# Stick-breaking attention in pairs of heads: both products of the next step made together, and a projection's chunk kept whole behind the turn of the weights

## The chip, the cores and the metric

The kernel runs on one core of a Trainium2 chip. The metric is the device time in microseconds of one launch, and the kernel before is given by the median of three timed runs, 2637.6 us.

## What is computed

The program is one inference step of a two-layer decoder trunk on 1024 prompt tokens and 8 x 4 sample tokens (T = 1056 columns), model width 1024, in float32. Layer 0 mixes tokens with a gated short convolution, layer 1 with stick-breaking attention (16 heads of 64), and each is followed by a convolutional feed-forward block. Only the attention of layer 1 is touched by the change. For one head it is, cut to what matters:

```python
z = q @ k.T / sqrt(64) + bias            # strictly causal: key s < query t
beta, keep = sigmoid(z), sigmoid(-z)
w[t, s] = beta[t, s] * prod(keep[t, j] for s < j < t)
o = w @ v                                # v, k, q are projections of the normalised x
```

## The kernel before, in words

Activations lie with features on partitions and tokens in columns. Every projection is computed in chunks of 352 tokens (TJ = 3 chunks for T). A matrix product in near-float32 precision takes three matmuls per 128 x 128 block of weights (`three`, lines 520, 523 and 524): high by high, low by high, high by low. GpSimd splits each weight tile into these two halves (lines 496 and 498), once the first matmul of the tile that is three places on has counted `w_used`.

The attention runs over 8 pairs of heads. For a pair there are 8 steps s (`STEPS`), one for each block of 128 queries, from the widest (1024 keys at s = 0) to the narrowest (128 keys at s = 7). A step of one head consists of

- `scores` on TensorE (line 705, with the diagonal mask, line 708),
- `sigmoids` on ScalarE, which make beta and keep for head 0 and then for head 1,
- `weigh(s, h)` on VectorE: a running product over keep from the right (a scan, line 1535), and its multiplication into beta (line 1539),
- `turn(s, u)` on TensorE, the transposition of the weights in PSUM (line 738); u = 0 is the first four blocks of keys, u = 1 the rest, which only the wide steps 0 to 3 have (`WIDE`),
- the copies out of PSUM: `copy_first` on ScalarE for u = 0, `copy_second` on VectorE for u = 1 (line 1518),
- `values(s, u)` on TensorE (line 767), the product with v.

TensorE is filled up by the projections of the pair that comes next: it has 9 chunks (`CHUNKS`: three of k, three of q, three of v), each 24 matmuls on eight blocks k = 0..7 of the features, all in PSUM bank 0, and one chunk is put into each step (the last two into step 7). VectorE moves each out of PSUM, scaled, by `take(after, n)` (lines 1507 and 1511), and counts `lin_taken`; the next chunk waits for that count.

All engines run the order in which their instructions are written. TensorE's order in a step s of `attend` is: `scores(s+1)`; `turn_v` for s = 0 or `values(s-1, 1)`; the first half of chunk s; `turn(s, 0)`; the second half of chunk s; `values(s, 0)`; `turn(s, 1)`. VectorE's is: `take(s-1)`; `copy_second(s-1)`; `weigh(s, 1)`; for s = 0 the two copies of v (`copy_v`, line 1524); `weigh(s+1, 0)`. So the product of head 1 of a step is made in the step itself, and that of head 0 one step earlier. `values(s-1, 1)` waits for the semaphore `second_copied`, `turn(s, 0)` for `weighed` of each head. In ScalarE's `sigmoids(s)` keep of head h waits for `scanned` of the same head one step earlier, because there is one buffer `keep` for each head, while beta has two for each.

The last pair (`attend_last`) has no next pair to project. Its steps are filled with the attention of the sample tokens, two samples in every two steps (`sample_scores`, `sample_weigh`, `sample_turn`, `sample_values`, `sample_out`, `sample_take`).

Of the kernel before, what the change touches and what calls it, by code (L numbers as in the profile page):

```python
# [23 lines left out]
KC = D // P  # L24
# [4 lines left out]
TJ = 3  # L29
# [61 lines left out]
H_SC_IN, H_SC_OUT, H_FFN0, H_QKV, H_WO, H_FFN1 = (BLOCKS * n for n in range(6))  # L91
# [15 lines left out]
FIRST_BANK = [0, 1, 2, 3, 4, 5, 0, 1, 2]  # L107
# [17 lines left out]
STEPS = QT  # L125
# [4 lines left out]
CHUNKS = 3 * TJ  # L130
# [43 lines left out]
def build(nc, x_in, weights, taps_sc, taps_ffn, state_sc, state_ffn, gains, bias_heads, bias_rows,  # L174
# [6 lines left out]
    with ctx:  # L181
# [110 lines left out]
        def projected(n):  # L292
            return bank[n // 3][:, n % 3, 0:TW]
# [23 lines left out]
        def sem(name):  # L317
            return ctx.enter_context(nc.semaphore(name))
# [31 lines left out]
        lin_taken = sem("lin_taken")  # L350
# [166 lines left out]
        def _(pe):  # L517
            def three(o, w, c0, hi, lo, first, last, counts=False):

                mm = nc.tensor.matmul(o, w_hi[w][:, c0:c0 + P], hi, start=first, stop=False)  # L520
                if counts:
                    mm.then_inc(w_used, 1)
                nc.tensor.matmul(o, w_hi[w][:, c0:c0 + P], lo, start=False, stop=False)  # L523
                return nc.tensor.matmul(o, w_lo[w][:, c0:c0 + P], hi, start=False, stop=last)  # L524
# [183 lines left out]
                    nc.tensor.matmul(score[h][:, width - P:width], ident_b[:, :], diag_b[:, :],  # L708
                                     start=False, stop=True).then_inc(scored, 1)

            def project(count, n, bank_n, half=None, h_base=None):

                w, j = n // TJ, n % TJ
                ring = (T_QKV + w) % SPLIT
                for k in range(KC) if half is None else range(half * KC // 2, (half + 1) * KC // 2):
                    if k == 0 and j == 0:
                        pe.wait_ge(w_split, count(3, T_QKV + w + (RAW + 1)))
                    if h_base is not None:
                        pe.wait_ge(h_ready, h_base + j * KC + k + 1)
                    mm = three(projected(bank_n), ring, k * P, h_hi[:, k, j * TW:(j + 1) * TW],  # L720
                               h_lo[:, k, j * TW:(j + 1) * TW], k == 0, k == KC - 1, j == k == 0)
                    if k == KC - 1:
                        mm.then_inc(lin_full, 1)
# [47 lines left out]
            def attend(count, after, par):  # L771

                for s in range(STEPS):
                    if s + 1 < STEPS:
                        scores(count, s + 1, par)
                    elif after is not None:
                        pe.wait_ge(lin_taken, after(CHUNKS, 2 * TJ))
                        scores(after, 0, 1 - par)
                    if s == 0:
                        turn_v(count)  # L780
                    elif WIDE[s - 1]:
                        values(count, s - 1, 1)
                    if after is not None:
                        pe.wait_ge(lin_taken, after(CHUNKS, s))
                        project(after, s, 0, 0)
                        if s == STEPS - 1:
                            project(after, s, 0, 1)
                    turn(count, s, 0)
                    if after is not None:
                        if s == STEPS - 1:  # L790
                            pe.wait_ge(lin_taken, after(CHUNKS, STEPS))
                            project(after, STEPS, 0)
                        else:
                            project(after, s, 0, 1)
                    values(count, s, 0)
                    if WIDE[s]:
                        turn(count, s, 1)

            first = pair_count(0)
            for n in range(CHUNKS):  # L800
                if n < RING:
                    pe.wait_ge(block_taken, TAKEN_FFN0 + BLOCKS - RING + n + 1)
                else:
                    pe.wait_ge(lin_taken, n - RING + 1)
                project(first, n, FIRST_BANK[n], None, H_QKV if n < TJ else None)
                if n == 0:
                    fold_mean(2, 1)
                    sum_four(2, QUADS - 1)
                if n == 1:
                    fold_mean(2, 2)  # L810
                if n == 2 * TJ:
                    pe.wait_ge(lin_taken, 2 * TJ)
                    scores(first, 0, 0)
# [447 lines left out]
        def _(dve):  # L1261
# [230 lines left out]
            def take(count, n, par, reuse):  # L1492

                j = n % TJ
                block = slice(j * TW, (j + 1) * TW)
                if reuse is not None and n == 0:
                    dve.wait_ge(k_stored, reuse(16, 16))
                    dve.wait_ge(k_copied, reuse(1, 1))
                if reuse is not None and n == TJ:
                    dve.wait_ge(q_copied, reuse(1, 1))  # L1500
                if reuse is not None and n == 2 * TJ:
                    dve.wait_ge(v_stored, reuse(16, 16))
                    dve.wait_ge(v_copied, reuse(1, 1))
                bank_n = 0 if reuse is not None else FIRST_BANK[n]
                dve.wait_ge(lin_full, count(CHUNKS, n + 1))
                if n // TJ == 1:
                    V.scalar_tensor_tensor(q_t[par][:, block], projected(bank_n), DH ** -0.5, rstd[:, block],
                                           ALU.mult, ALU.mult).then_inc(lin_taken, 1)
                else:
                    dst = k_t[par] if n < TJ else v_t  # L1510
                    V.tensor_tensor(dst[:, block], projected(bank_n), rstd[:, block], ALU.mult).then_inc(lin_taken, 1)
# [15 lines left out]
            def weigh(count, s, h):  # L1527
                n, width, w = 2 * s + h, WIDTH[s], beta[s % 2][h]
                dve.wait_ge(beta_done, count(PER_HEAD, n + 1))
                dve.wait_ge(keep_done, count(PER_HEAD, n + 3))  # L1530

                dve.wait_ge(weighed, count(PER_HEAD, n + 1))

                back = keep[h][:, width - 1:0:-1]
                V.tensor_tensor_scan(prod[:, width - 1:0:-1], back, back, 1.0,  # L1535
                                     ALU.mult, ALU.bypass).then_inc(scanned, 1)
                dve.wait_ge(scanned, count(PER_HEAD, n + 3))

                V.tensor_tensor(w[:, 0:width - 1], w[:, 0:width - 1], prod[:, 1:width],  # L1539
                                ALU.mult).then_inc(weighed, 1)  # L1540

            def attend(count, after, par):
                for s in range(STEPS):
                    if s and after is not None:
                        take(after, s - 1, 1 - par, count)
                    if s and WIDE[s - 1]:
                        copy_second(count, s - 1)
                    weigh(count, s, 1)
                    if s == 0:
                        copy_v(count)  # L1550
                    if s + 1 < STEPS:
                        weigh(count, s + 1, 0)
                    elif after is not None:
                        take(after, s, 1 - par, count)
                        weigh(after, 0, 0)
                        take(after, s + 1, 1 - par, count)

            first = pair_count(0)
            invert(2, 0)
# [8 lines left out]
            weigh(first, 0, 0)  # L1568
            for n in range(CHUNKS - 2, CHUNKS):
                take(first, n, 0, None)  # L1570
            with dve.Fori(0, (KC - 2) // 2) as i:
                for q in range(2):
                    attend(pair_count(i, q), pair_count(i, q + 1), q)
            attend(pair_count(KC - 2), pair_count(KC - 1), 0)

            def sample_q(bp):
# [34 lines left out]
            def attend_last(count):  # L1611
                V.memset(q_rows[:, :], 0.0).then_inc(made, 1)
                for s in range(STEPS):
                    bp = s // 2
                    if s and WIDE[s - 1]:
                        copy_second(count, s - 1)
                    weigh(count, s, 1)
                    if s == 0:
                        copy_v(count)
                        dve.wait_ge(made, 6)  # L1620
                        sample_q(0)
                    elif s % 2 == 0:
                        sample_take(bp - 1)
                        sample_q(bp)
                    if s + 1 < STEPS:
                        weigh(count, s + 1, 0)
                    if s % 2 == 0:
                        sample_weigh(bp)
                sample_take(NB // 2 - 1)
# [114 lines left out]
```

## Time and profile before

| | |
|---|---|
| timed runs | 2636.41, 2637.6, 2638.77 us |
| the profiled execution's own time | 2637.77 us |
| its span, first to last instruction | 2636.0 us |
| mean granted TensorE clock | 0.993 |
| busy in the span: TensorE, VectorE, ScalarE, GpSimd | 98%, 54%, 20%, 27% |
| attention stage, from the first scores to the last output of the samples | about 1193 to 1743 us |

The attention stage is one fifth of the span. Its first seven pairs repeat one pattern of about 66.7 us each; pair 4, from 1392.5 to 1459.3 us, stands for them. A matmul's record lasts longer than the time after which the next may start, so the distance from one start to the next start is what an instruction costs TensorE. Times are microseconds from the start of the span.

### The profile page before, as it was taken

The numbers are of one execution on the slowest core, as the hardware profiler recorded it, in microseconds if no ns is written. First come the engines' busy times: TensorE is split into PE (matmuls) and PEld (weight loads), VectorE is DVE, ScalarE is ACT, GpSimd is POOL, SyncE is SP. The second block draws the span as 40 slices with busy tenths as digits, with TensorE's granted clock in tenths as the row PEclk, the third lists the DMA queues.
The fourth block names the chain that finished last, engine by engine and source line by source line (L and its number), as shares of the span: only waits on it lengthen the run. The fifth ranks groups of instructions, "written<-read, shape, count | busy, mean of one in ns | idle before, by whom it ended". The sixth has DMA issues, their size and how long they took to land.

```text
span 2636.0 us, 40878 instructions
## 1 busy us (share of the span) xinstructions
PE 2577.5 (98%) x16934; PEld 2451.6 (93%) x16934; DVE 1423.8 (54%) x1430; ACT 533.9 (20%) x1081; POOL 719.0 (27%) x408
## 2 busy tenths in 40 slices
PE   7999999999999999999999999989999999999996
PEld 7999999999999999988888888669999999999995
DVE  8333446444444444466777777654644444444445
ACT  4000221000000000144444444432100000000012
POOL 4333333322322233321111111013233232223332
PEclk9999999999999999999999999999999999999998
DMA  4111111111111111121111111731111111111111
GB/s 141 42 48 48 47 43 49 46 43 48 48 33 48 48 48 48 52 97 59 42 41 41 41 41 41 240 123 41 49 48 41 48 48 33 48 49 48 48 44 67
DMA packets 62428, 149.07 MB, mean 57 GB/s; under 512 B 5570, under 2 KB 28866, under 8 KB 62274
## 3 DMA queue, kind: packets, MB, share of 16 engines
q1 hardware_dynamic: 56082, 130.35, 15.4%
q10 hardware_dynamic: 6192, 16.36, 1.6%
q8 instruction: 134, 2.20, 0.3%
q14 instruction: 20, 0.16, 0.0%
HBM read 128.91 MB, written 17.78 MB: 56 GB/s over the span
## 4 chain that ended last, share of the span: by engine, by line
PE 94%; DVE 4%; issue 1%; ACT 1%; DMA 0%; DVEq 0%; ACTq 0%
PE bank L520 28%; PE bank L524 28%; PE bank L523 28%; PE bank L767 3%; PE bank L705 3%; PE bank L738 2%; DVE total L1295 1%; DVE h_lo L1286 1%; PE bank L708 0%; DVE h_lo L1368 0%; PE bank L870 0%; DVE prod L1535 0%; DVE rstd L1300 0%; PE bank L839 0%; DVE y_rows L1362 0%
## 5 line engine op out<-in xcount | busy, mean ns | idle before, releaser
L520 PE MATMUL bank<-h_hi,w_hi 128*128 128x352 f32 x3648 | 1193.3, 327 | 18.9 <-DVE h_lo L1286 9.1
L524 PE MATMUL bank<-h_hi,w_lo 128*128 128x352 f32 x3648 | 1178.9, 323 | 0.0
L523 PE MATMUL bank<-h_lo,w_hi 128*128 128x352 f32 x3648 | 1173.6, 322 | 0.0
L496 POOL CAST w_hi<-raw 128x1024 fp32r<-128x1024 f32 x196 | 221.4, 1130 | 1861.8 <-PE bank L520 1817.7
L520 PEld LDWEIGHTS bank<-h_hi,w_hi 128*128 128x128 f32 x3648 | 686.3, 188 | 30.6 <-issue 20.5
L523 PEld LDWEIGHTS bank<-h_lo,w_hi 128*128 128x128 f32 x3648 | 690.5, 189 | 0.9 <-issue 0.2
L524 PEld LDWEIGHTS bank<-h_hi,w_lo 128*128 128x128 f32 x3648 | 688.0, 189 | 0.0
L498 POOL TENSOR_TENSOR w_lo<-raw,w_hi 128x1024 fp32r<-128x1024 f32 x196 | 486.9, 2484 | 15.7
L1422 DVE TENSOR_TENSOR x<-x,bank 128x1056 f32<-128x1056 f32 x174 | 218.2, 1254 | 321.9 <-PE bank L524 321.9
L520 PE MATMUL bank<-a_hi,w_hi 128*128 128x352 f32 x1056 | 343.4, 325 | 3.1 <-DVE x L1422 3.1
L523 PE MATMUL bank<-a_lo,w_hi 128*128 128x352 f32 x1056 | 340.7, 323 | 0.0
L524 PE MATMUL bank<-a_hi,w_lo 128*128 128x352 f32 x1056 | 340.6, 323 | 0.0
L1399 DVE TENSOR_TENSOR ext<-bank,rstd 128x1056 f32<-128x1056 f32 x44 | 55.4, 1258 | 340.5 <-PE bank L524 340.5
L520 PEld LDWEIGHTS bank<-a_hi,w_hi 128*128 128x128 f32 x1056 | 198.4, 188 | 10.5 <-DVE x L1344 4.0
L1535 DVE TENSOR_TENSOR_SCAN prod<-keep 128x895 f32<-128x895 f32 (+7 forms) x128 | 196.4, 1534 | 16.1 <-ACT keep L916 12.3
L916 ACT ACTIVATE smp<-ext 128x32 f32<-128x32 f32 x52 | 12.0, 231 | 942.3 <-DVE ext L1399 851.6
L523 PEld LDWEIGHTS bank<-a_lo,w_hi 128*128 128x128 f32 x1056 | 198.4, 188 | 0.3
L524 PEld LDWEIGHTS bank<-a_hi,w_lo 128*128 128x128 f32 x1056 | 198.4, 188 | 0.0
L916 ACT ACTIVATE beta<-bank,bias_pair 128x896 f32<-128x896 f32 (+7 forms) x128 | 94.9, 741 | 212.9 <-PE bank L708 208.9
L1539 DVE TENSOR_TENSOR beta<-beta,prod 128x895 f32<-128x895 f32 (+7 forms) x128 | 125.2, 978 | 4.4
L1374 DVE TENSOR_SCALAR y<-ext,tap_ffn 128x1024 f32<-128x1024 f32 x44 | 116.5, 2648 | 9.7 <-DVE ext L1399 9.6
L1381 DVE SCALAR_TENSOR_TENSOR y<-ext,tap_ffn,y 128x1024 f32<-128x1024 f32 x88 | 113.0, 1284 | 0.7 <-DVE y L1388 0.4
(123 smaller groups left out, 1641.7 us busy)
## 6 DMA issues: line engine op xcount, KB each, us to landing
raw<-weights SPq DMA_DIRECT2D x196, 512.0 KB, 3.5
x_spill<-x ACTq DMA_DIRECT2D x8, 528.0 KB, 6.1
k_out<-k_t ACTq DMA_DIRECT2D x8, 528.0 KB, 2.9
v_out<-v_t ACTq DMA_DIRECT2D x8, 528.0 KB, 2.7
x<-x_spill SPq DMA_DIRECT2D x8, 528.0 KB, 7.4
pages_hi<-cache_k SPq DMA_DIRECT2D x8, 512.0 KB, 6.3
pages_hi<-cache_v SPq DMA_DIRECT2D x8, 512.0 KB, 7.5
pages_lo<-cache_k SPq DMA_DIRECT2D x8, 512.0 KB, 7.3
```

The lines of the kernel that those rows point to most:

```text
L496: nc.gpsimd.tensor_copy(w_hi[ring][:, :], raw[slot][:, :]).then_inc(w_high, 1)
L498: nc.gpsimd.tensor_tensor(w_lo[ring][:, :], raw[slot][:, :], w_hi[ring][:, :].bitcast(f32), ALU.subtract).then_inc(w_split, 1)
L520: mm = nc.tensor.matmul(o, w_hi[w][:, c0:c0 + P], hi, start=first, stop=False)
L523: nc.tensor.matmul(o, w_hi[w][:, c0:c0 + P], lo, start=False, stop=False)
L524: return nc.tensor.matmul(o, w_lo[w][:, c0:c0 + P], hi, start=False, stop=last)
L705: nc.tensor.matmul(score[h][:, n0:n1], q_t[par][rows, i * P:(i + 1) * P], k_t[par][rows, n0:n1], start=True, stop=n1 < width)
L916: return nc.scalar.activation(o, i, func, **kw)
L1374: V.tensor_scalar(o[:, 0:SEQ], e[:, 0:SEQ], tap(0), None, ALU.mult).then_inc(tapped, 1)
L1381: main = V.scalar_tensor_tensor(o[:, 0:SEQ], e[:, n:n + SEQ], tap(n), o[:, 0:SEQ], ALU.mult, ALU.add)
L1422: V.tensor_tensor(xx, xx, result(s), ALU.add).then_inc(taken[s], 1)
L1535: V.tensor_tensor_scan(prod[:, width - 1:0:-1], back, back, 1.0, ALU.mult, ALU.bypass).then_inc(scanned, 1)
L1539: V.tensor_tensor(w[:, 0:width - 1], w[:, 0:width - 1], prod[:, 1:width], ALU.mult).then_inc(weighed, 1)
```

## The change

The functions named are those described above. In the diff `chunks` is the range of the blocks k of a chunk.

```diff
-            def project(count, n, bank_n, half=None, h_base=None):
+            def project(count, n, bank_n, chunks=range(KC), h_base=None):
...
-                for k in range(KC) if half is None else range(half * KC // 2, (half + 1) * KC // 2):
+                for k in chunks:
...
                     elif WIDE[s - 1]:
                         values(count, s - 1, 1)
-                    if after is not None:
+                    ahead = {0: 6, STEPS - 1: KC}.get(s, 0)
+                    if ahead:
                         pe.wait_ge(lin_taken, after(CHUNKS, s))
-                        project(after, s, 0, 0)
-                        if s == STEPS - 1:
-                            project(after, s, 0, 1)
+                        project(after, s, 0, range(ahead))
                     turn(count, s, 0)
-                    if after is not None:
-                        if s == STEPS - 1:
-                            pe.wait_ge(lin_taken, after(CHUNKS, STEPS))
-                            project(after, STEPS, 0)
-                        else:
-                            project(after, s, 0, 1)
+                    if s == STEPS - 1:
+                        pe.wait_ge(lin_taken, after(CHUNKS, STEPS))
+                        project(after, STEPS, 0)
+                    else:
+                        if not ahead:
+                            pe.wait_ge(lin_taken, after(CHUNKS, s))
+                        project(after, s, 0, range(ahead, KC))
                     values(count, s, 0)
...
             def attend(count, after, par):
                 for s in range(STEPS):
-                    if s and after is not None:
+                    if s:
                         take(after, s - 1, 1 - par, count)
                     if s and WIDE[s - 1]:
                         copy_second(count, s - 1)
-                    weigh(count, s, 1)
                     if s == 0:
                         copy_v(count)
                     if s + 1 < STEPS:
                         weigh(count, s + 1, 0)
-                    elif after is not None:
+                        weigh(count, s + 1, 1)
+                    else:
                         take(after, s, 1 - par, count)
                         weigh(after, 0, 0)
                         take(after, s + 1, 1 - par, count)
+                        weigh(after, 0, 1)
...
             weigh(first, 0, 0)
             for n in range(CHUNKS - 2, CHUNKS):
                 take(first, n, 0, None)
+            weigh(first, 0, 1)
...
                     if s and WIDE[s - 1]:
                         copy_second(count, s - 1)
-                    weigh(count, s, 1)
...
                     if s + 1 < STEPS:
                         weigh(count, s + 1, 0)
+                        weigh(count, s + 1, 1)
                     if s % 2 == 0:
                         sample_weigh(bp)
```

On VectorE `weigh(s+1, 1)` now follows `weigh(s+1, 0)` in step s, where `weigh(s, 1)` used to stand at the head of step s. On TensorE the chunk of a step is no longer halved around `turn(s, 0)`: in step 0 three quarters stand ahead of it and a quarter behind, in steps 1 to 6 the whole chunk stands behind, and step 7 is as before. In the last pair only VectorE's order changes.

## Rows read from the trace of the kernel before

**Rows 1.** Windows, pair 4: length, PE, PEld, DVE, ACT, POOL busy, clock, DMA, GB/s.

```profile
1392.60:1459.40 66.80, 66.12 (x508) 55.15 (x507) 49.56 (x52) 30.16 (x54) 11.75 (x6) 1.00 0.12 41
```

**Rows 2.** Waits of PE in 1192 to 1743: total us, times, longest.

```profile
PE bank L738 <- DVE v_rows L1524: 5.1, 8, 2.4
...
PE bank L738 <- DVE beta L1539: 2.3, 4, 0.9
...
PE bank L767 <- DVE w_second L1518: 0.2, 1, 0.2
```

**Rows 3.** Timeline of PE, pair 4: start, us, line, operation, count, idle before.

```profile
1406.30 0.40 PE L520 MATMUL bank<-h_hi,w_hi 128*128 128x352 f32 x1
...
1408.73 1.06 PE L738 MATMUL bank<-ident,beta 128*128 128x128 f32 x8 [0.28 <-DVE v_rows L1524]
...
1411.64 1.09 PE L767 MATMUL bank<-w_first,v_rows 128*64 128x128 f32 x16
...
1415.44 1.09 PE L767 MATMUL bank<-w_second,v_rows 128*64 128x128 f32 x16
...
1432.02 1.13 PE L705 MATMUL bank<-k_t,q_t 64*128 64x512 f32 x4
...
1441.25 0.44 PE L767 MATMUL bank<-w_second,v_rows 128*64 128x128 f32 x4
```

**Rows 4.** Windows of PE on one whole chunk and two halves.

```profile
1399.24:1403.30 4.06, 3.96 (x16) 1.00 0.00 0
1416.47:1418.49 2.02, 2.02 (x8) 1.00 0.03 8
1419.29:1421.37 2.08, 1.99 (x8) 1.00 0.00 0
```

**Rows 5.** Timeline of DVE, pair 4, steps 0 and 1.

```profile
1408.50 4.13 DVE L1535 TENSOR_TENSOR_SCAN prod<-keep 128x895 f32<-128x895 f32 x1
...
1413.68 0.52 DVE L1511 TENSOR_TENSOR k_t<-bank,rstd 128x352 f32<-128x352 f32 x1
1414.11 1.27 DVE L1518 COPY w_second<-bank 128x512 f32<-128x512 f32 x2
1415.31 2.01 DVE L1535 TENSOR_TENSOR_SCAN prod<-keep 128x895 f32<-128x895 f32 x1
1417.35 1.09 DVE L1539 TENSOR_TENSOR beta<-beta,prod 128x895 f32<-128x895 f32 x1
```

**Rows 6.** Timeline of ACT, pair 4: the first copy of step 0, keep of step 4.

```profile
1409.39 1.09 ACT L916 ACTIVATE w_first<-bank 128x512 f32<-128x512 f32 x2
...
1434.01 0.68 ACT L916 ACTIVATE keep<-bank,bias_pair 128x512 f32<-128x512 f32 x1
```

**Rows 7.** Timeline of POOL, pair 4.

```profile
1408.37 2.38 POOL L498 TENSOR_TENSOR w_lo<-raw,w_hi 128x1024 fp32r<-128x1024 f32 x1
1434.49 1.33 POOL L496 CAST w_hi<-raw 128x1024 fp32r<-128x1024 f32 x1 [23.73 <-PE bank L520]
1435.90 3.18 POOL L498 TENSOR_TENSOR w_lo<-raw,w_hi 128x1024 fp32r<-128x1024 f32 x1
```

**Rows 8.** Timeline of DVE, pair 4, the products of step 4, head 0.

```profile
1435.02 1.87 DVE L1535 TENSOR_TENSOR_SCAN prod<-keep 128x511 f32<-128x511 f32 x1
1436.93 2.70 DVE L1539 TENSOR_TENSOR beta<-beta,prod 128x511 f32<-128x511 f32 x1
```

**Rows 9.** Windows of PE around idle times: length, busy, granted clock, DMA, GB/s.

```profile
43.05:46.00 2.95, 0.00 (x0) 0.92 0.45 150
46.00:48.95 2.95, 2.92 (x8) 0.50 0.07 28
1674.60:1676.90 2.30, 0.00 (x0) 1.00 1.06 389
1676.90:1680.50 3.60, 3.55 (x28) 0.53 1.05 406
...
55.50:60.00 4.50, 3.02 (x19) 1.00 0.01 4
```

More of the change, by code:

```diff
@@ L804, in _ @@
                     pe.wait_ge(lin_taken, n - RING + 1)
-                project(first, n, FIRST_BANK[n], None, H_QKV if n < TJ else None)
+                project(first, n, FIRST_BANK[n], h_base=H_QKV if n < TJ else None)
                 if n == 0:
@@ L1552, in attend @@
                         weigh(count, s + 1, 0)
-                    elif after is not None:
+                        weigh(count, s + 1, 1)
+                    else:
                         take(after, s, 1 - par, count)
```

## The prediction

> **What bounds the kernel now.** I read the windows by pair first [rows 1]: in a pair of 66.8 us TensorE is busy 66.1 us at full clock and VectorE 49.6. So only time that TensorE stands still, or spends on its instructions, counts. VectorE has 17 us to spare on average, but the change moves work in its order, so the question is what is late, not how much is done. Next come TensorE's waits in the stage [rows 2]: the copies of v cost it 5.1 us in eight waits (the longest, 2.4, in the last pair), the weights' product 2.3 in four, and the second copies 0.2 in one. The last figure looks harmless. It is the one to follow up, because the diff puts something ahead of those copies. Last I read the timelines of one pair on all engines [rows 3, 5 to 8].
>
> **Step 0 on TensorE.** The half chunk begins at 1406.30 and costs 2.02 [rows 3, 4], so `turn(0, 0)` could start at 1408.32; it starts at 1408.73, held by the copies of v: 0.41 lost. VectorE makes `weigh(0, 1)` and then those copies in both orders, so v is ready at the same time. With six matmuls more ahead (2.02 / 12 each, with the ends of the chunk taken off some 0.97 in all) the turn starts at 1409.29, no wait left: -0.41. Behind it stand only six matmuls instead of twelve, and these cover ScalarE's first copies. In the trace they begin 0.66 after the turn and take 1.09 [rows 3, 6], so they would end at 1411.04, while `values(0, 0)` is due at 1411.64 - 0.41 = 1411.23. Covered by 0.19; without that cover up to 0.2 a pair.
>
> **Step 1, the second copies.** This is the main term. `values(0, 1)` on TensorE waits for both `copy_second(0)`. In the trace VectorE ends `weigh(1, 0)`, takes chunk 0 at 1413.68, copies from 1414.11 to 1415.38, and TensorE starts at 1415.44, 0.06 later [rows 3, 5]. The copies are on the path already, with hardly any slack. After the change `weigh(1, 1)` stands ahead of take and copies. It lasts from 1415.31 to the end of its product, 1417.35 + 1.09 = 1418.44, which is 3.06 from the start to where the next may begin (ends overlap by some 0.07) [rows 5]. Its keep exists by then: the scan of head 0 ran for 4.13 from 1408.50, and ScalarE's first copies, which follow that keep, began at 1409.39 [rows 5, 6]. So the three pieces only change places, the copies end at 1415.38 + 3.06 = 1418.44, and TensorE starts at 1418.50. It was due at 1415.44 - 0.41 = 1415.03 and stands idle 3.47 us. Together with step 0: **+3.06 a pair**. Behind the waiting `values` are queued `turn(1, 0)`, chunk 1 and the scores of step 3, and every other engine waits for those, so nothing gives this back within the pair. What goes, the wait of `turn(s, 0)` for the product of head 1, was worth nothing in these pairs: the four such waits [rows 2] all lie in the last one.
>
> **Steps 2 and 3.** The copies of steps 1 and 2 come after products that are now a step ahead, and a whole chunk lies between those products and the second turn. The products of two heads of 768 columns take about 5.4 (2.01 + 1.09 scaled by 767/895, twice), from 1418.4 to 1423.9; TensorE's turn, chunk and values in between take 0.8 + 4.06 + 1.0 after its own `values(0, 1)`, up to 1425.4. So the copies find VectorE free. No stall.
>
> **Step 4.** The split of the next tile starts on GpSimd 0.6 after the first matmul of chunk 3. Measured from the start of `scores(4)`, S = 1432.02, its cast is at S + 2.47 [rows 3, 7]; with `turn(3, 0)` ahead of the chunk (0.80 from start to start, 1418.49 to 1419.29 [rows 4]) it is at S + 3.27. In the trace VectorE and GpSimd hold each other up: the scan of 895 takes 4.13 beside GpSimd's subtraction of 2.38 and 2.01 without; the product of 511 takes 2.70 beside one that itself takes 3.18 [rows 5, 7, 8]. Scaled from 895 columns, undisturbed ones of 511 take 1.2 and 0.65. Keep of head 0 ends at S + 2.67 [rows 6]. One after the other: scan to 3.9, cast to 5.0, product to 5.5, subtraction to 7.8, scan to 8.9, product to 9.5, take and two copies (0.43 + 0.5) to 10.4. TensorE wants them at S + 9.23 - 0.04 = 9.2 [rows 3], so it waits **1.2**. If the two engines did not hold each other up, the copies would be done at about 8.8, ahead of need: 0. I take 1.2, because the rows show both engines stretched. The Trainium skill, "SBUF — State Buffer", section "SBUF: two separate sides", says that a VectorE operation with two SBUF inputs and a GpSimd operation exclude each other for a whole instruction, the first to start winning. By that rule this term is 1.2, without it 0, or 8 us over seven pairs; the stretched rows agree with the rule.
>
> **The chunk kept whole.** Two halves cost 2.02 + 2.08, a whole one 4.06 [rows 4]: -0.04 in each of steps 1 to 6, **-0.24** a pair (bounds 0 and -0.5, since the two halves differ by 0.06 between themselves and each step may win that and more). Chunk 7 and chunk 8 stand where they stood. The waits for `lin_taken` are met: chunk s - 1 ends at least two turns and a set of scores earlier, and its take stands behind only the short products in the narrow steps.
>
> **The clock.** TensorE's granted clock fell to half behind idle times of 2.3 us and more: idle 1674.60 to 1676.90, then 0.53 over 3.60 us; idle 43.05 to 46.00, then 0.50 over 2.95. From 55.50 to 60.00, with 1.48 us of idleness in it, it stayed at 1.00 [rows 9]. The new stall is 3.5 us in every pair, longer than all of these, so I expect 1.2 GHz for a while behind each. The two cases lost 2.95 x 0.50 = 1.5 and 3.60 x 0.47 = 1.7 of full-clock time. Bounds are 0 (no fall) and 3.3 (two falls a pair); I take the one behind the longer idle time, **+1.5**. The Trainium skill, "TensorE: Matmul & The Clock Gate", section "HAM oscillation — how this bites in real kernels", warns that idle gaps repeated in a loop make the clock fall again each time. By it the falls add 7 x 1.5 = 10.5 us; without it the sum would be 2665.
>
> **The last pair.** Here TensorE does wait for the product of head 1, 2.3 us in four waits [rows 2]. They go, but behind two of them ScalarE's copy of the sample weights is ready only at about the same time, and now the sample's product and the second copies wait behind one more `weigh`. In step 1 the second copies come some 0.2 later, behind the sample's product. From step 2 on TensorE's scores for the samples, which waited for `sample_take` behind `weigh(s, 1)`, no longer have that product ahead of them, and the turns of steps 3 and 5 no longer wait: about half of the 2.3 comes through. I take **-1.0**, bounds -2.3 (all four waits gone) and +1.7 (one more fall of the clock).
>
> **Sum.** A pair: 3.06 + 1.2 - 0.24 + 1.5 = 5.5; seven pairs 38.6; the last one -1.0; in all +37.6. On the profiled execution's own 2637.8 (span 2636.0 and 1.8 around it; the median of the runs is 2637.6, the same within 0.01%) that gives 2675.4, so 2675.
>
> **Rivals.**
> - The clock holds. For it: the other waits of these pairs never disturbed it. Against it: the rows behind 2.3 and 2.95 us. 2637.8 + 7 x 4.02 - 1.0 = 2665.
> - The wait of step 4 isn't there, because GpSimd falls between VectorE's operations otherwise than I laid it: 2667 with the clock's falls, 2656 without.
> - The clock falls twice a pair, or GpSimd's split also hits the products of step 2: 3.3 in place of 1.5, 2688.
> - Faster: the second copies do not hold TensorE. Then only the gains are left: 7 x (-0.41 - 0.24) - 1.0 = -5.6, 2632. The place is `values(0, 1)`, and it decides at 1415.03: the copies would have to end by then, so the 3.06 of `weigh(1, 1)` would have to be gone ahead of them. For it speaks only that VectorE is idle 17 us in a pair; against it that none of this idleness lies between 1408.50 and 1418.44.
> - The change does not do what it says, as VectorE is bound by keep and the products end where they ended: the loss then shrinks with the order's effect and the time stays near 2638. Against it: keep of step 1 is there before the scan of head 0 ends.
>
> **How the numbers follow.** Chances: forecast 0.55; clock holds 0.20; no wait in step 4 0.10; 2688 0.08; faster 0.05; no change 0.02. The range 2656 to 2686 leaves out the last three of these, 0.15, and holds the others. A change of 0.2%, 5 us, is what a measurement of this kernel can tell from none. Faster by more: 0.05; within: 0.02; slower by more: 0.93.
>
> **What would show it.** Behind the change: TensorE's waits for `copy_second` (line 1518's kind) at about 3.5 + 1.2 us a pair, some 33 us in the stage, in fourteen waits; those for the copies of v down to the last pair's; a granted clock below 1 in a stretch of some 3 us behind each long wait; pairs of about 72.2 us instead of 66.7; two GpSimd subtractions a pair overlapping VectorE's products. The prediction is wrong if the pairs stay at 67 us or less, or if the waits sit elsewhere.

## The result: 1.5% slower, and the profile after

The changed kernel takes 2674.86 us in the median of four runs (2670.60 to 2676.19); the kernel before, over its four runs, 2637.01 (2628.94 to 2638.77). The ratio is 1.0148, with an interval of 1.0137 to 1.0160. Forecast were 2675 us.

The windows of pair 4 before [rows 1] and now, with the same columns:

```profile
1409.40:1481.60 72.20, 67.09 (x508) 56.23 (x506) 49.98 (x52) 29.48 (x54) 11.51 (x6) 0.98 0.11 38
```

The same work stands in 72.2 us instead of 66.8, and the clock is below 1 for the first time in these pairs. TensorE's waits in the attention stage, 1192 to 1790 us, where [rows 2] stood before:

```profile
PE bank L767 <- DVE w_second L1520: 35.1, 16, 4.1
...
PE bank L520 <- DVE v_t L1513: 2.8, 7, 0.4
PE bank L738 <- DVE v_rows L1526: 2.4, 1, 2.4
```

Two of the three old entries have gone as far as they can: the wait for the product is not there, that for v is left in the last pair alone. In their place stands one that was 0.2 us, in the last pair alone, and it is 35.1, of which 33.2 us in fourteen waits are in the seven pairs. Its two places in pair 4, from TensorE's timeline:

```profile
1426.10 1.04 PE L738 MATMUL bank<-ident,beta 128*128 128x128 f32 x8
...
1430.07 1.56 PE L705 MATMUL bank<-k_t,q_t 64*128 64x512 f32 x8
1431.57 0.28 PE L708 MATMUL bank<-diag_b,ident_b 128*128 128x128 bf16 x2
1435.56 1.97 PE L767 MATMUL bank<-w_second,v_rows 128*64 128x128 f32 x16 [3.71 <-DVE w_second L1520]
...
1461.46 0.92 PE L705 MATMUL bank<-k_t,q_t 64*128 64x384 f32 x4
...
1463.60 0.44 PE L767 MATMUL bank<-w_second,v_rows 128*64 128x128 f32 x4 [1.00 <-DVE w_second L1520]
```

The turn at 1426.10 has no wait any more. The values at 1435.56 have one of 3.71, those at 1463.60 one of 1.00. VectorE at the first place shows why, where [rows 5] were the old order:

```profile
1425.36 4.15 DVE L1537 TENSOR_TENSOR_SCAN prod<-keep 128x895 f32<-128x895 f32 x1
1429.54 1.09 DVE L1541 TENSOR_TENSOR beta<-beta,prod 128x895 f32<-128x895 f32 x1
1430.73 2.02 DVE L1537 TENSOR_TENSOR_SCAN prod<-keep 128x895 f32<-128x895 f32 x1
1432.79 1.09 DVE L1541 TENSOR_TENSOR beta<-beta,prod 128x895 f32<-128x895 f32 x1
1433.80 0.52 DVE L1513 TENSOR_TENSOR k_t<-bank,rstd 128x352 f32<-128x352 f32 x1
1434.23 1.28 DVE L1520 COPY w_second<-bank 128x512 f32<-128x512 f32 x2
```

The turn that feeds these copies started at 1429.05, and in step 2 such copies begin 0.6 us after their turn (1443.79, 1444.38). Here two instructions of head 1's product and a take stand ahead of them, and VectorE is never idle. They end at 1435.51 and TensorE starts 0.05 later. The second place, VectorE and then GpSimd (compare [rows 7, 8]):

```profile
1456.06 1.22 DVE L1537 TENSOR_TENSOR_SCAN prod<-keep 128x511 f32<-128x511 f32 x1 [2.06 <-ACT keep L918]
1457.32 1.35 DVE L1541 TENSOR_TENSOR beta<-beta,prod 128x511 f32<-128x511 f32 x1
1458.77 3.22 DVE L1537 TENSOR_TENSOR_SCAN prod<-keep 128x511 f32<-128x511 f32 x1
1462.02 0.69 DVE L1541 TENSOR_TENSOR beta<-beta,prod 128x511 f32<-128x511 f32 x1
```

```profile
1456.65 1.47 POOL L496 CAST w_hi<-raw 128x1024 fp32r<-128x1024 f32 x1 [29.03 <-PE bank L520]
1458.20 2.71 POOL L498 TENSOR_TENSOR w_lo<-raw,w_hi 128x1024 fp32r<-128x1024 f32 x1
```

Two scans of one size take 1.22 and 3.22 us; the long one begins 0.57 into GpSimd's subtraction and ends about where a scan begun at the subtraction's end, 1460.91, would. And the windows on TensorE (length, busy, clock, DMA, GB/s) that answer to [rows 9]; the first two were asked of all engines and have their columns:

```profile
1431.80:1435.50 3.70, 0.05 (x1) 0.00 (x0) 3.67 (x6) 3.27 (x4) 0.00 (x0) 0.94 0.00 0
1435.50:1438.80 3.30, 3.24 (x25) 2.91 (x25) 3.16 (x4) 0.18 (x1) 0.00 (x0) 0.55 0.03 5
```

```profile
1216.90:1223.70 6.80, 6.50 (x35) 0.52 0.01 2
1506.90:1513.70 6.80, 6.11 (x33) 0.51 0.01 2
```

The clock falls behind every first stall: to 0.55 over 3.3 us in pair 4, and in pairs 1 and 5 it stays there over 6.8 us.

### The profile page after: what moved, and what is told of

The parts are those of the page before. It is cut to its first block, busy times and chain, and to the rows that moved or that the text cites. A ratio compares the mean times of both kernels' runs of the same rounds, so it can differ in the third digit from the quotient of the medians.

```text
span 2672.7 us, 40878 instructions
## 1 busy us (share of the span) xinstructions
PE 2583.4 (97%) x16934; PEld 2460.6 (92%) x16934; DVE 1426.5 (53%) x1430; ACT 529.8 (20%) x1081; POOL 716.9 (27%) x408
## 4 chain that ended last, share of the span: by engine, by line
PE 89%; DVE 8%; issue 1%; ACT 1%; DMA 0%; DVEq 0%; ACTq 0%
PE bank L520 27%; PE bank L524 27%; PE bank L523 27%; DVE prod L1537 3%; PE bank L767 3%; PE bank L705 2%; PE bank L738 2%; DVE total L1297 1%; DVE beta L1541 1%; DVE h_lo L1288 1%; DVE h_lo L1370 0%; DVE w_second L1520 0%; PE bank L708 0%; DVE rstd L1302 0%; PE bank L872 0%
## 5 line engine op out<-in xcount | busy, mean ns | idle before, releaser
L1537 DVE TENSOR_TENSOR_SCAN prod<-keep 128x895 f32<-128x895 f32 (+7 forms) x128 | 216.5, 1692 | 70.2 <-ACT keep L918 58.0
L1541 DVE TENSOR_TENSOR beta<-beta,prod 128x895 f32<-128x895 f32 (+7 forms) x128 | 106.2, 829 | 4.4
```

## The experiments

Two kernels take the change apart, two fill the idle time to weigh the clock (beside the changed kernel run a second time), two move GpSimd's split, and the last tries for a better version. All ratios are to the kernel before on the same chip.

### VectorE's order alone

```diff
 # TensorE as in the kernel before:
 project(after, s, 0, 0); turn(count, s, 0); project(after, s, 0, 1)
 # VectorE as in the changed kernel:
-weigh(count, s, 1)          # in step s
+weigh(count, s + 1, 1)      # in step s, behind weigh(s + 1, 0)
```

> Only VectorE's order is changed; TensorE keeps its two half chunks around each turn. Theory (the second copies of step 0 stand behind weigh(1, 1) and hold TensorE, whatever stands around the turns): the stall at values(0, 1) is 3.1 us (due at 1415.44 instead of 1415.03), the one of step 4 about 1 us, the clock falls once a pair: pairs of about 72.2 us, 2675 us within 4. Rival (the loss comes from the chunk being put whole behind the turn): near 2638.

Measured: 2679.53 us, ratio 1.0182 (1.0165 to 1.0199). TensorE's waits in its seven pairs (1192 to 1700 us):

```profile
PE bank L767 <- DVE w_second L1518: 29.3, 14, 3.3
```

The same fourteen waits, two a pair, with the old halves of the chunk around the turn. The rival, that the whole chunk behind the turn makes the loss, would have given 2638: it is out. The time is half a microsecond above the range I gave, and the excess over the kernel before beside it, 2632.28, is 47 us where the forecast meant 37. The seven pairs take 510.7 us, 3 more than the changed kernel's: the clock stays low over 6.8 us in three of them instead of two, and the chunks are still halved, so the 0.24 us a pair is not won. The rest of the difference is not traced to a place.

### TensorE's order alone

```diff
 # TensorE as in the changed kernel:
 turn(count, s, 0); project(after, s, 0, range(ahead, KC))
 # VectorE as in the kernel before:
 weigh(count, s, 1)          # in step s
```

> Only TensorE's order is changed; VectorE makes weigh(s, 1) in step s as before, in the last pair too. Theory: turn(s, 0) then stands directly behind values(s-1, 1) and waits for weigh(s, 1), which begins only when the copies that release those values end: some 2.1 us in step 1, 1.9 in step 2, 1.7 in step 3, 2 in step 4, together 7 to 8 a pair and so 2688 to 2700 us, waits named after the product (line 1539's kind) and not after the second copies. Rival (the whole chunk is harmless or useful by itself): 2632 to 2638.

Measured: 2658.20 us, ratio 1.0097 (1.0080 to 1.0114). The waits of the seven pairs:

```profile
PE bank L738 <- DVE beta L1541: 18.9, 28, 1.4
PE bank L767 <- DVE w_second L1520: 3.9, 7, 0.8
```

The mechanism is mainly the one I named, four waits for the product in each pair, though one for the second copies stands beside them, which I had ruled out. The size is not mine: I had put 7 to 8 us a pair and 2688 us at least, and the pairs are 70.2 us, 3.5 more. The timeline of step 1 shows what I left out:

```profile
1426.40 0.66 PE L738 MATMUL bank<-ident,beta 128*128 128x128 f32 x4
1428.43 0.66 PE L738 MATMUL bank<-ident,beta 128*128 128x128 f32 x4 [1.37 <-DVE beta L1541]
```

The four transposes of head 0 do not wait, only those of head 1 do. The waits shrink from step to step, 1.37, 0.55, 0.43, 0.31 in steps 1 to 4; I read this as a wait in one step delaying TensorE against VectorE, so that the next is shorter, which no run tests by itself. Neither half of the change is good alone, and the two do not add up: together they lose 38 to 40 us, and alone 47 and 26.

### The idle time filled, 24 matmuls

```diff
                     elif WIDE[s - 1]:
+                        if s == 1:
+                            for _ in range(24):
+                                nc.tensor.matmul(attended[:, 0:P], ident[:, :], ident[:, :], start=False,
+                                                 stop=False, skip_group_check=True)
                         values(count, s - 1, 1)
```

> The changed kernel with 24 matmuls of the identity, 128 x 128 in float32, put on TensorE ahead of values(0, 1) of every pair with a next one; they add into columns of PSUM that the values of step 3 overwrite, so nothing of the result changes. At 0.13 us each, as the transposes of this size stand from start to start, they fill 3.1 of the 3.7 to 4.1 us in which TensorE is idle. Theory (idleness makes the granted clock fall, and that costs about 1.5 us a pair): the clock stays at 1.00 in pairs 1 to 7, the pairs are 70.7 instead of 72.3 us, 2664 us. Rival (the slow stretch behind the stall has another cause, or costs nothing because VectorE is late anyway): 2675 as the changed kernel, or more, if the matmuls push values back.

Measured: 2675.02 us, ratio 1.0161 (1.0143 to 1.0180), the rival's time. But the timeline says that the test was spoilt:

```profile
1431.17 5.58 PE L784 MATMUL bank<-ident 128*128 128x128 f32 x48
1436.67 1.09 PE L767 MATMUL bank<-w_second,v_rows 128*64 128x128 f32 x16
```

24 matmuls leave 48 records and take 5.5 us, not 3.1. The second copies had ended at 1434.98, so the values were pushed back 1.7 us. The clock was at 1.00 in all seven pairs. A gain of about 1.5 us a pair and a loss of 1.7 look like nothing; by the time alone the wrong theory would have won.

### The changed kernel again, and 14 matmuls

> The changed kernel itself once more, as the one that the next three stand beside: 1.0148 of the kernel before, about 2671 to 2675 us.

Measured: 2674.05 us, ratio 1.0153 (1.0140 to 1.0167).

```diff
-                            for _ in range(24):
+                            for _ in range(14):
```

> As the kernel with 24 matmuls of the identity ahead of values(0, 1), but with 14. The run with 24 showed each to stand as two of 0.114 us, 5.5 us in all, 1.7 more than the stall it was to fill, so it pushed values back by what the clock gave. 14 of them take 3.2 us, less than the stall of 3.8. Theory (the slow clock behind the idle time costs 1.5 us a pair): clock 1.00, values(0, 1) starts as late as in the changed kernel, pairs of 70.8 us instead of 72.3, 11 us less than the changed kernel beside it. Rival (the clock is lowered but VectorE is what is late, so it costs nothing): the same time as the changed kernel.

Measured: 2659.33 us, ratio 1.0102 (1.0086 to 1.0119): 14.7 us less than the changed kernel beside it, where I had given 11; 13.1 of it lie in the seven pairs. The first stall of pair 4, and a whole pair in the windows (length, busy, clock, DMA, GB/s), with the pair of the changed kernel run beside it last:

```profile
1427.03 3.34 PE L784 MATMUL bank<-ident 128*128 128x128 f32 x28
1430.87 1.09 PE L767 MATMUL bank<-w_second,v_rows 128*64 128x128 f32 x16 [0.50 <-DVE w_second L1524]
```

```profile
1404.85:1475.59 70.74, 68.85 (x534) 1.00 0.11 38
```

```profile
1412.24:1484.37 72.13, 67.04 (x506) 0.98 0.11 38
```

The values start as late as ever, still behind the copies, and with useless matmuls in the gap the pair is shorter. So the slow clock had a price of its own. It is shown in kernels that differ in nothing else: 1.4 to 1.6 us in an ordinary pair, and more in the pairs in which the clock stays low longer, 1.9 on the mean of seven (from the first scores to the last pair's, 507.6 against 494.4 us).

### GpSimd's split moved, twice

```diff
+            COUNT_AT = (2, 1, 1)
...
-                               ..., k == 0, k == KC - 1, j == k == 0)
+                               ..., k == 0, k == KC - 1,
+                               k == 0 and j == (0 if first pair else COUNT_AT[w]))
```

> The changed kernel with one thing moved: in the attention the count that lets GpSimd split the next weight tile is made by the first matmul of chunks 2, 4 and 7 instead of 0, 3 and 6 (the first pair's own projection is left as it is). Theory (GpSimd's split holds VectorE's scan of step 1 up by 2.1 us and its products of step 4 by 2.9): the second copies of step 0 end 2.1 us earlier, the stall at values(0, 1) shrinks from 3.5 to 1.3 us, too short for the clock to fall, the stall of step 4 goes; a pair of 66.73 - 0.41 + 1.3 - 0.24 = 67.4, in all 2641 us. Rival (the scan's 4.13 us are its own, or other work makes it long): stalls and time as in the changed kernel, 2675.

Measured: 2655.48 us, ratio 1.0091 (1.0074 to 1.0108), between theory and rival. VectorE's scan of step 1, and the values of steps 1 and 3 on TensorE:

```profile
1415.44 2.01 DVE L1539 TENSOR_TENSOR_SCAN prod<-keep 128x895 f32<-128x895 f32 x1
```

```profile
1423.51 1.09 PE L770 MATMUL bank<-w_second,v_rows 128*64 128x128 f32 x16 [1.57 <-DVE w_second L1522]
...
1442.93 0.66 PE L770 MATMUL bank<-w_second,v_rows 128*64 128x128 f32 x8 [1.62 <-DVE w_second L1522]
```

The scan takes 2.01 instead of 4.15 with nothing changed but when GpSimd works, the first stall is 1.57, and the clock does not fall behind it. (In the seven pairs it fell once, over 3.4 us, behind the 1.60 us stall of step 3 in pair 7.) What I missed is a stall of 1.62 at `values(2, 1)`, in a step that had none. The split now stood beside the products of step 3:

```profile
1437.45 3.47 DVE L1539 TENSOR_TENSOR_SCAN prod<-keep 128x639 f32<-128x639 f32 x1
```

Undisturbed it takes 1.5. The delay had been moved. The next kernel puts it behind those products:

```diff
-            COUNT_AT = (2, 1, 1)
+            COUNT_AT = ((KC - 1, 2), (0, 1), (0, 1))     # (k, j) for the tiles of k, q and v
```

> The changed kernel with GpSimd's splits counted by the last block of chunk 2 (k = 7) and by chunks 4 and 7. The run with chunks 2, 4 and 7 showed the stall of step 1 at 1.6 instead of 3.5 us, but the split that now met the products of step 3 gave 1.7 at values(2, 1). Theory (what the split meets is held up, wherever it stands): here it starts after the products of step 3, the wait at values(2, 1) goes, only the 1.6 of step 1 stays, pairs of 66.73 - 0.41 + 1.6 - 0.24 = 67.7, about 5 us above the kernel before. Rival: the second wait is of another cause and stays, 14 to 20 us above.

Measured: 2642.91 us, ratio 1.0034 (1.0022 to 1.0046), 8.7 us above the kernel before beside it. The only wait for the second copies left in its seven pairs is that of step 1:

```profile
PE bank L770 <- DVE w_second L1522: 11.4, 7, 1.9
```

Pairs are 67.5 us, 0.2 less than I gave, but in pair 1 this wait is 1.9 us and the clock fell behind it, over 3.4 us, and the last pair has a wait of 1.2 us for a page of the cache. I had counted neither. So of the 40 us by which the changed kernel stands above the kernel before on this chip, 31 depend on when GpSimd's split meets VectorE's products, with the order of both other engines left as the change has it. This counts in the falls of the clock that came with the longer stalls.

### A hybrid

```diff
 # the kernel before, and
+                cut = 6 if n == 0 else KC // 2       # blocks of the chunk ahead of the turn
 # the counts (KC - 1, 2), (0, 1), (0, 1) for GpSimd, and VectorE's new order in the last pair only
```

> The kernel before with three things that the runs point to: three quarters of chunk 0 ahead of turn(0, 0), GpSimd's splits counted as in the run with chunk 2's last block, 4 and 7, and in the last pair alone VectorE's order of the changed kernel. The theory gives 0.41 us a pair from the wait for v, which the undisturbed scan of step 1 lets through, and 1 to 2.3 us in the last pair: 4 to 5 us less than the kernel before, 0.15 to 0.2%. Rival (in the pairs with a projection the order of before has nothing left to win, the gain at v is lost at the turn of step 1): 1 to 2 us less, not to be told from none.

Measured: 2631.81 us against 2634.24 of the kernel before beside it, ratio 0.9993 (0.9984 to 1.0001). Its waits for v in the seven pairs are gone and the pairs are 66.2 us instead of 66.7 (pair 4 from 1389.64 to 1455.88), a little more than the 0.41 that was expected; from the first scores to the last pair's it is 462.4 us against 466.6 in the profile before, 4.2 less. The 1 to 2.3 us in the last pair did not come: it takes 83.7 us against 83.9, and TensorE waits 1.7 us for a page of the cache there. The median is lower, but the interval reaches 1: I can't call it faster.

## Why the prediction was right, point by point

The forecast was +5.5 us a pair, and pair 4 came out at 72.1 against 66.7 us, +5.4 (scores of step 1 to the next pair's, 1420.52 to 1492.59 and 1403.67 to 1470.37). Its terms, each from start to start in pair 4:

- **Step 0, forecast -0.41.** From the first scores of step 1 to where `values(0, 1)` was due: 1415.44 - 1403.67 = 11.77 before, 1430.07 + 1.76 - 1420.52 = 11.31 now. -0.46. The turn finds v ready and ScalarE's first copies stay covered.
- **Step 1, forecast 3.47.** Due at 1431.83, started at 1435.56: 3.73. The three pieces changed places as said. The 0.26 more is partly the scan of head 1, which begins 1.19 behind the start of the product ahead of it (1429.54, 1430.73), where a take begins after 1.01 (1432.79, 1433.80): in the program a scan waits for the semaphore `weighed` of the product ahead of it, and I had taken the 1.01 for both.
- **Steps 2 and 3, forecast none.** None.
- **Step 4, forecast 1.2, ends 0 and 1.2.** Due at 1461.46 + 1.07 = 1462.53, started at 1463.60: 1.07. The order of the pieces on the two engines was right to the piece.
- **The whole chunk, forecast -0.24.** Steps 1 (taken from the kernel with 14 matmuls, where the clock is full), 2, 3, and 4 to 6 together are 0.02, 0.07, 0.05 and 0.13 shorter: -0.27.
- **The clock, forecast +1.5, ends 0 and 3.3.** In pair 4 it is 1.4, by the kernel with 14 matmuls (72.13 against 70.74). Mis-sized was the mean: two pairs of seven had the long slow stretch, so the seven pairs grew by 41 us instead of 38.6.
- **The last pair, forecast -1.0, ends -2.3 and +1.7.** It is 81.5 us from its first scores to the first subtraction behind it, and was 83.8: -2.3. The waits did not shrink in sum. Those for the product went, 2.3 us, and ScalarE's sample weights (0.4 to 1.6) and the second copies (0.2 to 1.9) took all of it (I had named both, but the copies at 0.2). What was won in this execution is the clock: before it fell three times in the pair, once over twice the length, and the fall at 1690.8 to 1694.1, worth 1.65 us, is not there now. So the sign was right, for the wrong reason. And the size is one draw of several: in the second run of the changed kernel the last pair takes 79.5 us. Both have the same wait of 2.4 us for v in it. In the first run the clock fell behind it, in the second it did not (length, busy, clock, DMA, GB/s; the first run above, the second below):

```profile
1714.50:1716.90 2.40, 0.02 (x1) 1.00 1.04 394
1718.30:1721.80 3.50, 3.50 (x63) 0.51 1.06 400
```

```profile
1717.30:1719.70 2.40, 0.02 (x1) 1.00 1.05 394
1719.70:1726.70 7.00, 7.00 (x107) 1.00 1.08 384
```

The two errors, +2.6 on the seven pairs and -1.3 on the last, partly cancel, which is why the sum fits better than its terms. That is luck: the second run's last pair would have made the latter -3.3. The profiled execution's span grew by 36.7 us, 39 of it from the attention stage; 1.2 us of that was won back ahead of the stage and 1.0 behind it, both at places the change does not touch.

Of the two pages that the prediction drew on, the Trainium skill's "SBUF — State Buffer", section "SBUF: two separate sides", gave the rule by which step 4 came out, where a scan takes 3.22 us beside the subtraction and 1.22 ahead of it; the kernels with the split moved agree, with 2.01 us for the scan of step 1, which takes 4.15 beside the split. The Trainium skill's "TensorE: Matmul & The Clock Gate", section "HAM oscillation — how this bites in real kernels", warned of idle gaps repeated in a loop; here the clock fell behind each of the seven gaps of 3.7 to 4.1 us, and behind none of the same gaps when they were filled. The prediction's "2.3 us and more" is not a limit that the runs bear out: the clock fell behind all seven stalls of 3.2 us in the kernel with VectorE's order alone, but also behind one of 1.9 and one of 1.6 us in the two kernels with the split moved, and not behind every one of 2.4.

What stays open: what decides, beside the length of a gap, whether the clock falls; why it stays low over 6.8 us in pairs 1 and 5 and 3.4 in the others; and whether the hybrid is faster.

## What to carry to other kernels

When an edit moves work earlier on an engine with time to spare, don't ask whether the engine has the time; ask what it does in the order next, and who waits for that. A releasing instruction with 0.06 us between its end and its waiter's start is on the path, even if the table of waits shows nothing for it: the 0.2 us there [rows 2] came from the last pair. And a stall can cost more than its length, since the clock can be lost behind it: fill a test's gaps with care, measure what the filler takes, and count the two effects apart.

## What the runs showed of the hardware that was not expected

- A float32 matmul of 128 x 128 against 128 columns, all full, leaves two records and takes 0.23 us from start to start (24 in 5.5 us), while a transposition of the same size leaves one and takes 0.13 (eight in 1.02). The values of one turn, eight matmuls in 16 records, had shown it before.
- Useless matmuls of 3.3 us in a gap made the kernel 14.7 us faster, 0.55%. In the seven pairs, where 13.1 us of it lie, the granted clock was at 1.00 throughout, and the values behind the gap started no earlier.
- VectorE's scan or product and GpSimd's cast or subtraction delayed each other in both directions, and the delay went with the split to whatever products it met: 2.1 us of a scan of 895 in step 1, 2.0 of one of 639 in step 3, 2.0 of one of 511 in step 4.
- Two executions of one kernel differ in where the clock falls: behind the same idle 2.4 us of the last pair it fell in one and not in the other, and the last pair took 81.5 and 79.5 us.
